# Down-projection weights requested by ScalarE through its own DMA queue, gate/up weights by SyncE

## The reference

```python
h = rms_norm(x, ffn_norm_g)                       # 256 x 1024
top_w = softmax(top_k(h @ router_w + router_b, 4))
# for each expert e, on the tokens routed to it:
gu = xb @ w_gu[e] + b_gu[e]                       # w_gu[e]: 1024 x 2048
g, u = min(gu[:, :1024], 7), clip(gu[:, 1024:], -7, 7)
a = (u + 1) * (g * sigmoid(1.702 * g))
y = a @ w_dn[e] + b_dn[e]                         # w_dn[e]: 1024 x 1024
x = rms_norm(x + weighted scatter of y, final_norm_g)
```

## Time and profile before

| what | value |
|---|---|
| median of 3 runs | 1247.95 us (1245.55 to 1248.2) |
| the profiled execution's own time | 1247.7 us |
| its span, first to last instruction | 1245.9 us |
| TensorE busy | 1180.8 us (95%) |
| ScalarE busy | 254.9 us (20%) |
| moved by DMA over the span | 456.40 MB |

### The profile page before, as it was taken

One profiled execution on the slowest core, in us unless ns is written; L12 is line 12 of the kernel. 1 busy time (PEld: TensorE's weight loads), 2 busy tenths in 40 slices (PEclk: granted clock), 3 DMA queues, 4 the chain that ended last, 5 costly groups with the idle time before them and its releaser, 6 DMA issues.

```text
span 1245.9 us, 14242 instructions
## 1 busy us (share of the span) xinstructions
PE 1180.8 (95%) x6203; PEld 605.9 (49%) x6203; DVE 268.5 (22%) x536; ACT 254.9 (20%) x533; POOL 211.7 (17%) x90
## 2 busy tenths in 40 slices
PE   6999999999999999999999999999989999999986
PEld 6989877899433343333333333333333333333322
DVE  3146243222421112111111111111111111111112
ACT  6455456334210011010001000000100000000002
POOL 5866755686200000000000000000000000000000
PEclk9999999999999999999999999999999999999989
DMA  9754533499699999999999999999999999999993
GB/s 312 248 173 148 174 136 135 145 350 392 267 419 436 423 435 429 428 427 429 431 429 432 433 430 427 431 429 433 428 431 429 427 433 425 429 429 433 429 428 152
DMA packets 60663, 456.40 MB, mean 366 GB/s; under 512 B 5065, under 2 KB 33513, under 8 KB 43192
## 3 DMA queue, kind: packets, MB, share of 16 engines
q1 hardware_dynamic: 60600, 455.47, 88.5%
HBM read 454.39 MB, written 1.07 MB: 366 GB/s over the span
## 4 chain that ended last, share of the span: by engine, by line
PE 63%; DMA 33%; DVE 1%; ACT 1%; POOL 1%; issue 0%; SPq 0%; DVEq 0%; ACTq 0%; POOLq 0%
PE ps L526 61%; DMA arena<-in_expert_w_gate_up 32%; POOL w_parts L512 1%; PE ps L815 1%; DMA arena<-in_w_mem_kv 1%; PE ps L809 1%; ACT arena L1005 0%; ACT x_normed L1160 0%; DVE neg_max L1291 0%; ACT w_parts_odd L985 0%; PE ps L533 0%; PE ps L629 0%; DVE arena L1343 0%; PE ps L606 0%; DVE arena L1352 0%
## 5 line engine op out<-in xcount | busy, mean ns | idle before, releaser
L526 PE MATMUL ps<-arena,gathered_T 128*64 128x512 f32 x2048 | 477.5, 615 | 40.8 <-DMA arena<-in_expert_w_gate_up 40.8
L526 PE MATMUL ps<-arena 128*64 128x512 f32 (+6 forms) x1666 | 342.5, 537 | 2.2 <-ACT arena L1132 0.9
L526 PEld LDWEIGHTS ps<-arena,gathered_T 128*64 128x64 f32 x2048 | 146.6, 141 | 311.8 <-issue 276.1
L526 PEld LDWEIGHTS ps<-arena 128*64 128x64 f32 (+3 forms) x1666 | 135.7, 154 | 198.9 <-issue 193.3
L512 POOL TENSOR_TENSOR w_parts<-arena,w_parts 128x1024 fp32r<-128x1024 f32 x42 | 103.4, 2485 | 50.8 <-ACT w_parts L985 40.4
L512 POOL TENSOR_TENSOR w_parts_odd<-arena,w_parts_odd 128x1024 fp32r<-128x1024 f32 x38 | 90.9, 2413 | 48.2 <-ACT w_parts_odd L985 48.2
L1395 DVE TENSOR_SCALAR arena<-arena 128x128 f32<-128x128 f32 x64 | 19.3, 343 | 324.3 <-PE ps L809 324.3
L1124 ACT COPY arena<-ps 128x256 f32<-128x256 f32 x32 | 11.9, 372 | 372.2 <-PE ps L809 372.2
L1401 DVE TENSOR_SCALAR arena<-ps 128x512 f32<-128x512 f32 x32 | 22.1, 692 | 273.4 <-PE ps L526 273.4
L526 PEld LDWEIGHTS ps<-arena,x_normed 128*128 128x128 f32 x512 | 59.5, 191 | 26.0 <-issue 24.3
L1115 ACT ACTIVATE gathered_T<-ps,g_cols 128x128 f32<-128x128 f32 x128 | 36.5, 368 | 172.3 <-PE ps L526 172.3
(11 more groups left out here) (174 smaller groups left out, 720.3 us busy)
## 6 DMA issues: line engine op xcount, KB each, us to landing
arena<-in_expert_w_gate_up SPq DMA_DIRECT2D x56, 4096.0 KB, 39.3
arena<-in_expert_w_down SPq DMA_DIRECT2D x64, 2048.0 KB, 39.5
arena<-in_expert_w_gate_up SPq DMA_DIRECT2D x16, 2048.0 KB, 11.5
arena<-in_w_in SPq DMA_DIRECT2D x29, 1024.0 KB, 5.1
arena<-in_w_mem_kv SPq DMA_DIRECT2D x4, 1024.0 KB, 11.8
arena<-in_w_out SPq DMA_DIRECT2D x4, 1024.0 KB, 10.7
arena<-t_scratch SPq DMA_DIRECT2D x6, 384.0 KB, 3.8
arena<-in_w_branch_a SPq DMA_DIRECT2D x2, 1024.0 KB, 4.9
```

What stands on the lines that cost most here:

```text
L526: return nc.tensor.matmul(out, lhsT, rhs, start=start, stop=stop, **kw)
```

## The change

`load_weights` gets the engine that requests as an argument and moves out of SyncE's block, so that ScalarE can call it. The transfers of down weights of experts 4 to 31 (28 experts, two transfers each) leave SyncE's loop. ScalarE requests them instead, dn(n)a and dn(n)b at the head of its iteration n, with the same waits on `chunk_used` as SyncE had. Slots, order of use, waits of TensorE and all arithmetic stay.

```diff
+DOWN_BY_ACT = [c for c, (e, j, _) in TRANSFERS.items() if j >= KC and e >= FIRST_LONG]
 ...
+        def load_weights(eng, e, j, m, r):
+
+            if j < KC:
+                src = w_gu[bass.ds(e, 1), :, j * CHUNK:(j + m) * CHUNK].rearrange("o p c -> (o p) c")
+            else:
+                src = w_dn[bass.ds(e, 1), :, (j - KC) // 2, :].rearrange("o p c -> (o p) c")
+            eng.dma_start(ring[:, r:r + m, :].rearrange("p r c -> p (r c)"), src).then_inc(landed[r], 16)
+
         @block.sync
         def _(sp):
-            def load_weights(e, j, m, r):
-
-                if j < KC:
-                    src = w_gu[bass.ds(e, 1), :, j * CHUNK:(j + m) * CHUNK].rearrange("o p c -> (o p) c")
-                else:
-                    src = w_dn[bass.ds(e, 1), :, (j - KC) // 2, :].rearrange("o p c -> (o p) c")
-                sp.dma_start(ring[:, r:r + m, :].rearrange("p r c -> p (r c)"), src).then_inc(landed[r], 16)
-
...
             for c, (_, _, m) in TRANSFERS.items():
                 if c < RING:
                     continue
+                if c in DOWN_BY_ACT:
+                    continue
                 sp.wait_ge(chunk_used, NF + c - RING + m)
-                load_weights(*TRANSFERS[c], ring_slot(c))
+                load_weights(sp, *TRANSFERS[c], ring_slot(c))
...
             for n in range(EXPERTS):
+                for c in DOWN_BY_ACT:
+                    e, j, m = TRANSFERS[c]
+                    if e == n:
+                        act.wait_ge(chunk_used, NF + c - RING + m)
+                        load_weights(act, e, j, m, ring_slot(c))
                 if n:
                     move_weights(n - 1, (n - 1) % 2)
```

More of the change, by code:

```diff
@@ L497, in _ @@
                         for j in range(0, EXPERT_CHUNKS, 2):
-                            load_weights(e_b, j, 2, ring_slot(j))
+                            load_weights(sp, e_b, j, 2, ring_slot(j))
             for tt in range(T):
```

## The result

The change makes the kernel slower by 0.4%: 1251.55 us median (1250.73 to 1253.6, 8 runs) against 1246.41 (1245.55 to 1248.2, 8 runs), ratio 1.0041 with a 95% interval of 1.0031 to 1.0051. The direction was forecast; the size is 5.1 us where some 13 were forecast. The eight runs put the median of before 1.5 us under the 1247.95 us of three runs from which the forecast started. The profiled execution took 1250.73 us with a span of 1248.9, 3.0 over the span of before. It lies 0.8 us under the median of its kernel, and the profiled one of before 1.3 us over its own; these two make up the 2.1 us between 3.0 and 5.1.

The account below looks back on a forecast made before the run. Transfers at 430 GB/s bound the kernel, TensorE being 2.8 us an expert faster. gu(31)b landing at 1220.4 + 25.0 + 2.7 + 10.8 gave span 1258.9, +13.0, hence 1261 us; 8-in-10 range 1248 to 1271.

Parts of the forecast that it names:

- nothing is lost in the middle: Experts before the end: later gate/up costs no time, since TensorE has 2.8 us an expert to spare.
- T: End of the weight transfers: landing of the last one, dn(31)b, forecast to stay at 1227.3 us.
- dn(n) arrives long before its use: Expert stage: down weights in their own queue land some 15 and 26 us after request instead of 40.
- Requests on ScalarE cost nothing: Head of each ScalarE iteration: a request takes 0.33 us, hidden; even 7.21 us would be covered by idle time and slack.
- Sharing by packets in turn: DMA engines alternate packets between queues, giving gate/up two thirds and down one third; chance 0.40, time 1261 us.
- the rival of equal halves: DMA engines share equally by bytes, so gu(31)b lands last: +19.9 us, 1268 us; chance 0.23.
- dn(30)a is requested after two chunks, s + 3.5: Near the end, s being TensorE's start of gu(30)a: down takes 29.25 us, just a period, so ScalarE's queue never empties.
- the 6.85 us of dn(30): Near the end, at s + 12.2: work of dn(30) still to come, 9.75 less 2.9 us already served.
- the 2.7 us of slow products after the wait: TensorE at gu(31)b: after a wait of 4.7 us its products take 2.7 us longer (9.81 against 7.09).
- Order kept: Both queues served in the order of requests, as if one: 1248 us, no change; chance 0.12.
- More bytes a second: Two queues raise the transfer rate from 360 us on, each 1% giving 8.6 us; 1241 us at 440 GB/s; chance 0.08.
- A lower rate by changing queues: Switching queues lowers the transfer rate by 1%, +8.6 us on either sharing, 1270 to 1277; other slower cases together 0.17.

Follow-up runs that it names:

- last_four_back: The changed kernel with the down weights of experts 28 to 31 requested by SyncE again: 1246.69 us, ratio 1.0001 to the kernel before.
- from_20: The changed kernel with ScalarE requesting down weights from expert 20 on instead of from expert 4: 1257.39 us, ratio 1.0086 to the kernel before.
- last_two_only: The changed kernel with ScalarE requesting only the four down transfers of experts 30 and 31, SyncE all others: 1262.83 us, ratio 1.0130 to the kernel before.
- last_short_after: The changed kernel (two queues) with gate/up of expert 31 alone in transfers of 2 chunks (16 KB packets): 1259.41 us, ratio 1.0101 to the kernel before.
- equal_packets: The changed kernel with every gate/up transfer of 2 chunks, so packets of both queues have 16 KB: 1265.71 us, ratio 1.0157 to the kernel before.

## Why the prediction was right in direction and wrong in size

**What bounds the kernel, and that nothing is lost in the middle:** right. 430 GB/s in both kernels, T at 1226.5 in after (dn(31)b, requested at 1200.2, landed 26.3 us later) against 1227.3. TensorE waited 44.5 us in all for gate/up instead of 40.8, and now for the second transfer of an expert, as in the rows at 1183.92 and 1213.14. "dn(n) arrives long before its use" failed once, by the 1.7 us at 1196.15. The waits for gate/up began later than forecast (0.5 us of the 44.5 fell before 600 us, where they were expected from about 520), for the reason that follows.

**Requests on ScalarE cost nothing:** right, as far as the times can show. They took 0.33 us (0.33 to 0.44 over 56), and the copy that follows, now L1127, still idled about 10 us for TensorE. last_four_back agrees.

**Sharing by packets in turn:** right, and against the rival of equal halves. Gate/up transfers of 4096 KB landed 14.6 us apart beside 16 KB packets, and, when their own packets had 16 KB, transfers of 2048 KB landed 9.8 us apart, 19.5 us for 4096 KB.

**The step that failed** is "dn(30)a is requested after two chunks, s + 3.5; at a third of the rate dn takes 29.25 us, just a period, so ScalarE's queue is never empty" and the 6.85 us of dn(30) taken from it as still to come. It treats the queue as having nothing waiting in front of dn(30) and serving it from the moment of the request. At a third of the rate down is served every 29.25 us, but up to about 600 us TensorE took 26.47 to 27.5 us for an expert and down was requested at that pace. The queue grew by the difference at each expert. The DMA view of after has the first down request on ScalarE (427.16 us), the one at 590.18 and dn(30)a at 1176.89:

```profile
arena<-in_expert_w_down ACTq DMA_DIRECT2D x1, 2048.0 KB, 18.1
...
arena<-in_expert_w_down ACTq DMA_DIRECT2D x1, 2048.0 KB, 31.8
...
arena<-in_expert_w_down ACTq DMA_DIRECT2D x1, 2048.0 KB, 33.8
```

The first request found its queue empty. Its 18.1 us are 3.6 us without a packet of its own (from 427.2 to 430.7 us the DMA view lists packets of q1 alone), then 14.5 at a third of the rate. From there the time grew to 31.8, some 2.3 us an expert over six experts. Once the transfers set the pace, requests and service had one period and the backlog stayed, to the end: 33.8. Since a third of the rate is just what down needs, nothing pulls the two queues together again or apart. So down ran less far ahead of gate/up than the sum had it, and gu(31)b landed 13.4 us before T instead of 6.9. With T itself 0.8 us earlier that makes 1213.1 for 1220.4, 7.3 us.

The size of this can be worked out. What stands ahead of dn(30)a at its request is served at a third of the rate, so a third of that time is work that comes on top of the prediction's 6.9 us between gu(31)b and T. In after 6.9 + 19.2/3 = 13.3 us, 13.4 measured; in from_20 6.9 + 5.0/3 = 8.6 us, 9.1 measured (1226.7 less 1217.6).

The rows of before held a sign of it that the prediction did not use: on one queue, too, requests in the stage where TensorE was faster took longer and longer to land, from 14.5 us at 389.65 to 40 us after 638. The 14.5 us are moreover not a backlog ahead of that transfer, as the prediction has it: 9.75 us of them are the transfer itself.

The second term off was the 2.7 us of slow products after the wait. The wait was 2.9 instead of 4.7 us, and the products took 0 and 1.7 us more in the two profiles, the latter at a granted clock of 0.50. 7.3 + 2.7 = 10.0 is what lies between the forecast span of 1258.9 and 1248.9.

The first of the two is the one that is due to the failed step. from_20 and last_two_only, where the queue starts late and nearly empty, came out at +10.6 us and +15.5 us of span. The backlog's growth is read from the trace; that it is what made after cheap is shown by from_20, since nothing else differs there but where ScalarE begins. last_two_only agrees, but there dn(29) stays in SyncE's queue, ahead of gu(31), so more than the backlog differs.

**The other rivals.** Order kept: out, by the landings. More bytes a second: out, 430 in both. A lower rate by changing queues: out, for these packets.

## What to carry to other kernels

In these runs, with the DMA engines full, a second queue changed no rate, only who was served first, and each queue got a share in proportion to its packet size. Give the transfers that are needed next the larger packets or the same queue; what is moved ahead is paid for at the end, where no later work hides it. Find the end by taking, for each of the last transfers, its landing plus everything queued behind its wait, and look in that queue for work that doesn't need the transfer. And a queue's backlog at the end is made by the stages before: work it out from where requests come faster than its share serves them.

## What the runs showed of the hardware

- Two hardware queues with work are served by packets in turn, a packet being one partition's piece of a transfer: in after the landings of gate/up (32 KB packets, 4096 KB) beside down (16 KB packets) are 14.6 us apart, which is two thirds of the rate; with 16 KB in both queues, transfers of 2048 KB land 9.8 us apart in each (last_short_after), against 4.88 us of work.
- A request on a queue with nothing in flight had its first packet 3.4 to 3.6 us later, in after (427.16), last_two_only (1172.27) and equal_packets (1184.27), while the other queue kept the engines busy. In after, requests that found work ahead of them on their queue landed 14.6 us behind it, with no such gap. Why is not shown.
- Gate/up in transfers of 2048 KB with 16 KB packets instead of 4096 KB with 32 KB moved 428 GB/s instead of 430. No run tells the packet size from the number of transfers.
- After a wait of TensorE of 2.88 us, 32 products took 7.09 us at a granted clock of 1.00 (after); after 2.70 us they took 8.78 in another execution of the same program, with the clock at 0.50 for a part of them; after 3.53 us 10.06 (last_two_only) and after 4.78 us 9.81 (before), both with a stretch at 0.50.
